# A hybrid decoder step on one core: GpSimd's low parts in two halves, and a pass's last group begun with products made ahead

## The reference, cut to what matters

```python
h2 = rmsnorm(x, g_ffn)
x = x + jnp.square(jax.nn.relu(h2 @ w_ff1)) @ w_ff2
return rmsnorm(x, g_final), s5_re, s5_im, gla_s
```

## Time and profile before

| | us |
|---|---|
| median of 3 runs | 2792.2 (2789.92 to 2797.39) |
| the profiled execution, its own time | 2799.96 |
| its span, first to last instruction | 2797.2 |
| TensorE matmul busy | 2681.8 (96%) |
| TensorE weight loads busy | 2513.9 (90%) |
| VectorE busy | 1915.2 (68%) |
| GpSimd busy | 1582.4 (57%) |
| ScalarE busy | 1125.8 (40%) |

### The profile page before, as it was taken

One profiled execution on the slowest core, in us unless ns is written; L12 is line 12 of the kernel. 1 busy time (PEld: TensorE's weight loads), 2 busy tenths in 40 slices (PEclk: granted clock), 3 DMA queues, 4 the chain that ended last, 5 costly groups with the idle time before them and its releaser, 6 DMA issues.

```text
span 2797.2 us, 44337 instructions
## 1 busy us (share of the span) xinstructions
PE 2681.8 (96%) x16558; PEld 2513.9 (90%) x16558; DVE 1915.2 (68%) x3321; ACT 1125.8 (40%) x1950; POOL 1582.4 (57%) x1205
## 2 busy tenths in 40 slices
PE   6999999997999999999999999999999998999997
PEld 4778887786999999999989999989999998999997
DVE  8856566463512666657467877878888779887876
ACT  4212321422232223142255445565555456555544
POOL 3534543564545343355447766766776666776673
PEclk9989999999999999999999999999999999999998
DMA  4455556866455545886234444565455666555554
GB/s 146 158 147 132 133 152 219 248 170 199 142 125 122 132 112 170 235 262 160 75 94 135 138 138 136 136 214 160 147 147 155 173 186 203 141 159 151 156 160 129
DMA packets 280516, 440.40 MB, mean 157 GB/s; under 512 B 27088, under 2 KB 167280, under 8 KB 280176
## 3 DMA queue, kind: packets, MB, share of 16 engines
q1 hardware_dynamic: 190448, 271.29, 33.0%
q0 software_dynamic: 34816, 67.12, 11.2%
q10 hardware_dynamic: 55040, 99.18, 10.9%
HBM read 381.32 MB, written 123.28 MB: 180 GB/s over the span
## 4 chain that ended last, share of the span: by engine, by line
PE 76%; DVE 11%; DVEq 4%; issue 4%; DMA 3%; ACT 1%; ACTq 1%; SPq 0%
PE ps L918 23%; PE ps L920 23%; PE ps L919 22%; DVE r_h L2279 4%; DVE f_h L2279 2%; PE ps L1097 1%; DVEq L2987 1%; DMA f_g<-x_scratch 1%; DVE f_z L2279 1%; DVEq L2982 1%; DVE f_g L2279 1%; PE ps L1182 1%; PE ps L1215 1%; DVEq L2977 1%; DVE r_m L2279 1%
## 5 line engine op out<-in xcount | busy, mean ns | idle before, releaser
L919 PE MATMUL ps<-r_h,w_hi 128*128 128x348 f32 (+3 forms) x2632 | 896.1, 340 | 0.0
L851 POOL TENSOR_TENSOR w_hi<-w_raw,zero 128x512 fp32r<-128x512 f32 x200 | 253.4, 1267 | 717.7 <-PE ps L920 683.1
L908 POOL TENSOR_TENSOR w_lo<-f_g,w_hi 128x512 fp32r<-128x512 f32 x336 | 468.3, 1396 | 221.7 <-ACT w_hi L1930 221.0
L908 POOL TENSOR_TENSOR w_lo<-w_raw,w_hi 128x512 fp32r<-128x512 f32 x336 | 464.4, 1385 | 218.4 <-ACT w_hi L1930 217.4
L918 PE MATMUL ps<-r_h,w_hi 128*128 128x512 f32 (+3 forms) x1520 | 532.9, 351 | 19.7 <-DVE r_h L2279 14.4
L920 PE MATMUL ps<-r_h,w_lo 128*128 128x512 f32 (+3 forms) x1520 | 528.6, 348 | 0.0
L919 PEld LDWEIGHTS ps<-r_h,w_hi 128*128 128x128 f32 x2632 | 500.0, 190 | 28.4 <-issue 0.7
L918 PE MATMUL ps<-r_o,w_hi 128*128 128x348 f32 (+1 forms) x1344 | 437.8, 326 | 19.2 <-issue 10.6
L920 PE MATMUL ps<-r_o,w_lo 128*128 128x348 f32 (+1 forms) x1344 | 433.8, 323 | 0.0
L2279 DVE TENSOR_TENSOR f_z<-f_z,ps 128x348 f32<-128x348 f32 (+3 forms) x704 | 346.3, 515 | 94.6 <-PE ps L920 93.3
L918 PE MATMUL ps<-r_z,w_hi 128*128 128x352 f32 (+3 forms) x1120 | 378.6, 338 | 12.8 <-DVE f_h L2279 10.8
(11 more groups left out here) (376 smaller groups left out, 4330.2 us busy)
## 6 DMA issues: line engine op xcount, KB each, us to landing
w_raw<-wpack SPq DMA_DIRECT2D x344, 256.0 KB, 2.8
f_g<-wpack SPq DMA_DIRECT2D x144, 256.0 KB, 2.7
w_raw<-up_sums SPq DMA_DIRECT2D x102, 256.0 KB, 2.6
f_g<-down_sums SPq DMA_DIRECT2D x102, 256.0 KB, 2.7
up_sums<-wpack POOLq DMA_DIRECT2D x48, 512.0 KB, 6.9
down_sums<-wpack POOLq DMA_DIRECT2D x48, 512.0 KB, 7.9
f_g<-up_sums SPq DMA_DIRECT2D x90, 256.0 KB, 2.7
w_raw<-down_sums SPq DMA_DIRECT2D x90, 256.0 KB, 2.7
```

What stands on the lines that cost most here:

```text
L851: pool.tensor_tensor(w_hi[:, s, :], rw, zero[:, :].to_broadcast([P, WB]), ALU.subtract).then_inc(w_high, 1)
L908: pool.tensor_tensor(w_lo[:, s, :], raw(s), w_hi[:, s, :].bitcast(F32), ALU.subtract).then_inc(w_split[s], 1)
L919: pe.matmul(out, wh, l, start=False, stop=False, skip_group_check=more)
```

## The change

Three things change.

- GpSimd's low part of a feed-forward block is made by two operations on 256 columns each; the second raises `w_split`. The mixer's `split` stays as it is.
- In each pass's `("down", 7, 0)`, TensorE first makes quad 14's share of products 1, 5 and 2 (`down_ahead`), and the steps of these three products then add quad 15's share alone. In the order of the steps, products 1, 5 and 2 are the first, second and fourth; they use the blocks 0, 1 and 3 of the item. The number of matmuls is the same.
- For quad 15, VectorE makes the low part of product 1 right behind the first mix, and ScalarE makes the second high part ahead of the last square.

```diff
+LAST_GROUP, AHEAD = ("down", FF_GROUPS - 1, 0), (1, 5, 2)
...
             for f in range(PASSES * PASS_BLOCKS):
                 s = f % RING
                 pool.wait_ge(w_high, HALVES * MIXER_BLOCKS + f + 1)
-                pool.tensor_tensor(w_lo[:, s, :], raw(s), w_hi[:, s, :].bitcast(F32), ALU.subtract
-                                   ).then_inc(w_split[s], 1)
+                for c in (0, WB // 2):
+                    last = pool.tensor_tensor(w_lo[:, s, c:c + WB // 2], raw(s)[:, c:c + WB // 2],
+                                              w_hi[:, s, c:c + WB // 2].bitcast(F32), ALU.subtract)
+                last.then_inc(w_split[s], 1)
...
+            def down_ahead(p, item, j):
+
+                (g, d), n, f = item[1:], HALF_TOKENS[p], item_at(p, item) + j
+                s, v = f % RING, ORDER[j]
+                name = {1: "a", 5: "c", 2: "b"}[v]
+                pe.wait_ge(w_split[s], (HALVES * MIXER_BLOCKS + f) // RING + 1)
+                pe.wait_ge(v_low, STEPS7 * up_count(p, 2 * g) + STEPS7)
+                for z in range(2):
+                    bank_free((p, item, z, name))
+                    out, w, q = bank_of((p, item, z, name))[:, 0:n], 2 * z * P, 2 * g
+                    three(out, w_hi[:, s, w:w + P], w_lo[:, s, w:w + P],
+                          ra[:, hid_hi(q, v):hid_hi(q, v) + n], ra[:, hid_lo(q, v):hid_lo(q, v) + n], True, False, more=True)
...
                 pe.wait_ge(w_split[s], (HALVES * MIXER_BLOCKS + f) // RING + 1)
+                ahead = item == LAST_GROUP and v in AHEAD
+                if item == LAST_GROUP and j == 0:
+                    for first in AHEAD:
+                        down_ahead(p, item, ORDER.index(first))
                 if d == 0:
                     pe.wait_ge(v_low, STEPS7 * up_count(p, 2 * g + 1) + j + 1)
                 for z in range(2):
                     out = bank_of((p, item, z, name))[:, 0:n]
                     if v in (1, 5, 2):
-                        bank_free((p, item, z, name))
+                        if not ahead:
+                            bank_free((p, item, z, name))
...
-                    for y in range(2):
+                    for y in (1,) if ahead else (0, 1):
...
                                 elif item == last_up and j == 6:
+                                    hidden_high(p, q, 1)
                                     square(p, q, 2)
-                                    hidden_high(p, q, 1)
...
                     if last_up:
-                        for x in (0, 1, 2, 4):
+                        for x in (0, 4, 1, 2):
                             hidden_part(p, q, x)
```

More of the change, by code:

```diff
@@ L1296, in down_product @@
                                      ra[:, hid_hi(q, v):hid_hi(q, v) + n], ra[:, hid_lo(q, v):hid_lo(q, v) + n],
-                                     y == 0 and v in (1, 5, 2), y == 1, more=v not in (1, 5, 2))
+                                     y == 0 and v in (1, 5, 2), y == 1, more=ahead or v not in (1, 5, 2))
                     if z == 0:
```

## The result

The changed kernel took 2769.88 us in the median of 6 runs (2766.85 to 2775.83), the kernel before 2792.3 in 6 runs beside it. The ratio is 0.9918, with a 95% interval of 0.9902 to 0.9935: 22.4 us faster. The forecast was 13.2 us faster, 2779.0 us; the measured time lies in its range.

What follows compares the result with a forecast made beforehand. TensorE, busy for 96% of the span, was taken as the bound, so only its waits can be won. The terms -8 - 4 - 2.5 + 1.3 = -13.2 us took the median from 2792.2 to 2779.0 us, range 2767 to 2794.

Steps and rivals of the forecast that it cites:

- Part 1: GpSimd's feed-forward low parts: two halves cost 0.15 us more, 1.44 a block (1.73 with a VectorE turn), hidden below TensorE's 1.91.
- Part 2: VectorE's low parts blocked by GpSimd: each waits at most half of 1.44 us, so up to 0.7 us sooner.
- The term "-8": 21 "down" items at groups 0 to 6: VectorE's additions start sooner; two thirds of upper bound 12.0, so -8 us.
- The term "-4": "Up" items, nine waits for VectorE's f_h, 8.3 us in all: 0.45 us less each, -4 us, bounds 0 and -6.
- The term "-2.5": Pass starts, six waits for r_h, 7.6 us in all: a third gained, -2.5 us, bounds 0 and -5.
- Part 3: Each pass's last group: TensorE does 12 matmuls, then waits 3.9 us for block 3; sum +1.3 us, bounds -2 and +4.5.
- the price of the clock: Last groups: half clock for 6.8 us behind the wait costs 2.7 us a pass, taken as unchanged.
- the likeliest case: The forecast with its own bounds, part 2 from -7 to -19 and part 3 from -2 to +4.5: 2769 to 2789 us.
- The halves don't help: Rival: GpSimd's two halves are served as one, VectorE gets in only behind the second; about 2794 us, chance 0.17.
- GpSimd becomes the bound: Rival: GpSimd's low parts decide from 1.91 us a block on; at 2.03, +80 us, about 2870; chance 0.06.
- The last group is filled: Rival: block 3 is ready in time, so most of the last groups' waits and low clock go; 2761 us, chance 0.05.
- The gain is halved: Rival: the gain is there but halved (-7), and the last group costs its upper bound (+4.5); 2789 to 2790 us, chance 0.12.

Runs made afterwards that it cites:

- the first experiment: The kernel before with GpSimd's feed-forward low parts in two halves and nothing else: 2766.09 us, ratio 0.9896 to the kernel before.

## Why the prediction was right, and where its sizes were off

**Part 1, the cost of the halves: right.** An undisturbed half takes 0.73 us and two that follow each other 1.44, as the sum had it: their ends overlap. A pair in GpSimd's timeline, and the means with VectorE's turns in them:

```profile
1834.74 1.44 POOL L910 TENSOR_TENSOR w_lo<-f_g,w_hi 128x256 fp32r<-128x256 f32 x2 [0.56 <-ACT w_hi L1952]
...
L910 POOL TENSOR_TENSOR w_lo<-f_g,w_hi 128x256 fp32r<-128x256 f32 x672 | 561.5, 858 | 112.9 <-ACT w_hi L1952 110.5
L910 POOL TENSOR_TENSOR w_lo<-w_raw,w_hi 128x256 fp32r<-128x256 f32 x672 | 552.0, 844 | 120.7 <-ACT w_hi L1952 119.7
```

That is 1.70 us a block (1.39 before), below 1.91, and it was hidden as forecast. The estimate from the Trainium skill's GPSIMD Engine Reference, section 3.1, was 1.47 for a pair; this trace has 1.44.

**Part 2, what VectorE gains: the mechanism right, two of three terms too small.** The operations named there, before and after:

```profile
L2279 DVE TENSOR_TENSOR r_h<-f_h,r_o 128x348 fp32r<-128x348 f32 x224 | 230.2, 1033 | 2.8 <-ACT r_o L2011 2.6
```

```profile
L2301 DVE TENSOR_TENSOR r_h<-f_h,r_o 128x348 fp32r<-128x348 f32 x224 | 165.9, 742 | 2.3 <-ACT r_o L2033 1.5
```

- The term "-8" for the 21 "down" items: measured -14.1. Its own upper bound was 12.0 for 21 x 0.57; I had taken two thirds of it because later passes have more waits ahead. That discount was the mistake: the items had lost 0.63, 0.67 and 0.73 us each in the mean of the three passes, not 0.57, and kept none of it in any pass.
- The term "-4" for f_h: measured -10.0, beyond its bound of -6. It was made as 0.45 us for each of nine waits, though "each has one to four such blocked operations ahead", as the prediction says itself, and each of them can gain; how much of the miss this is was not measured apart. Nor does a wait's own figure hold the slow matmuls behind it: the "up" items lost 14.7 us where the nine waits stand with 8.3.
- The term "-2.5" for pass starts: measured -1.4, and between -1.7 and +0.9 in the other kernels with halves; without halves, in the new order with three ahead, it is -2.9, so the column moves without them. By pass the change is 8.1 to 5.9, 8.6 to 9.2 and 8.6 to 8.6 us. The one gain is the granted clock of the first 20 us, which also differs between kernels with halves (with none or one ahead this item loses 8.1 us as before). The same stretch before and changed:

```profile
1430.00:1440.00 10.00, 9.39 (x37) 8.17 (x37) 3.96 (x4) 4.93 (x8) 5.82 (x4) 0.66 0.28 79
...
1430.00:1440.00 10.00, 6.38 (x38) 5.81 (x38) 6.33 (x7) 6.99 (x12) 5.28 (x7) 1.00 0.34 97
```

  The reason given there, that finer turns don't lessen the sum of both engines' work where VectorE never pauses, was right, and should have been followed to nothing.

The turns themselves can be counted. Before, 189 low parts of 348 or 344 columns began while a GpSimd low part was running; they ended 0.37 to 0.38 us behind its end, and the longest took 1.66 us. In the changed kernel 207 began so and ended 0.37 to 0.45 us behind the end of that half, and the longest took 1.07.

**Part 3, the last group: the chain and the waits right, the price of the clock not.** Block 3 was forecast ready 5.8 us behind TensorE's last matmul of the item before, with a wait of 3.9 us; it was 3.84. The sum said +1.3 (bounds -2 and +4.5), measured -1.8. The waits did what it said: 10.6 us before, 3 x 3.84 = 11.5 now, so +0.9. The price of the clock, which the prediction left "unchanged", is the term that was off: half clock stood behind the waits for 6.8 us in each pass before, and for 3.4, 6.8 and 6.8 us now, and in the second and third pass 1.4 and 1.7 us of that fell on the wait itself (0.8 to 1.0 before). That is 4.4 us less work at half clock, worth some 2.2. A wait of 0.6 us in the second pass's ("up", 15) is gone too. Why the stretch was shorter in the first pass, behind a wait of the same 3.84 us, no run shows. What the prediction didn't ask is what this part costs beside the halves alone, and there it is plain: +4.4 us by the table, 18.4 against 14.0. By the table, the halves were worth -31 us in all places, the new order beside them -5.5, and three products ahead instead of none +10.

**The sum.** In the terms' order: -14.1, -10.0, -1.4, -1.8, together -27; forecast -8, -4, -2.5, +1.3. The kernels' medians differ by 22.4. The 5 us between are the mixer's scatter as far as the profile shows; that is argued, not shown.

That the time fell in the range is partly luck. Part 2 gained 14.1 + 10.0 + 1.4 = 25.5 us, outside the -7 to -19 that the range was made from, and those bounds were narrower than the terms' own (12.0, 6 and 5 make 23); the 2769 of the likeliest case doesn't come out of them either (2792.2 - 19 - 2 = 2771). The whole 27 us would have given 2765, below the range's 2767. What was right is the mechanism, and the sign and place of the gain; the size was half of what the network gained.

**The rivals.** "The halves don't help" falls with the first experiment. "GpSimd becomes the bound" was false for halves at 1.70 us a block and true for quarters at 1.98; its threshold, 1.91, lies between the two, and no run is nearer to it. "The last group is filled" did not come true: with three products ahead 18.4 us stay lost there, with two 8.0, where none ahead has 8.5. "The gain is halved" did not either: part 2 alone gained 25.5.

## What to carry to other kernels

Where two engines take turns by whole operations, the length of an operation on the idle one is a delay for the busy one. Cutting it in two cost GpSimd 0.15 us a block (0.31 with VectorE's turns in it) and gave about 1% of the kernel; cutting it in four lost it all, because GpSimd's time for a block, 1.98 us, went above the 1.91 us of the bound engine: work out that pace first.

Work pulled ahead to fill a wait must not need anything that comes later than what was awaited. Go through every semaphore of the moved work; here two products had nothing new to wait for, and the third hung on a ring slot that had only just been released.

When a change has several parts, price each against the others, not against the kernel before: the halves had already taken from the last group what the products ahead were meant to fill.

## What the runs showed of the hardware that was not expected

A GpSimd operation of 512, 256 or 128 columns (two float32 inputs) that meets no VectorE operation takes 1.29, 0.73 and 0.46 us; with VectorE's turns in it, the last takes 0.55 in the mean. From the first two, 0.17 us is fixed. VectorE gets its turn between two GpSimd operations even where they are queued back to back: none of the 207 low parts counted above waited for a second half. An operation with an input in PSUM doesn't wait: before, 356 such additions of 348 columns began while GpSimd's low part was running, and they took 0.50 to 0.52 us.

Waits of the same length were not always followed by the same clock. Behind the changed kernel's three waits of 3.84 us it was half for 3.4 us in the first pass and for 6.8 in the other two; with two products ahead the same two waits in each pass were followed by 3.4 us at half clock in the first pass and by none in the others. With none or one product ahead, where no wait there was longer than 1.5 us, it was not halved in any last group. So a wait's price can't be read from its length alone: the start-to-start time of the item has both.
